# Expert rows with stationary blocks read at a step of two elements, in a fused transformer kernel

## The reference, cut to what matters

```python
expert = (i1 * N_SUB_KEYS + i2)                       # 128 experts for each token, out of 16384
a = jnp.einsum('cd,ced->ce', xb, u_tab[eb])           # up: token . u row
w = gb * jax.nn.gelu(a, approximate=False)            # gate times gelu
out = jnp.einsum('ce,ced->cd', w, v_tab[eb])          # down: sum of v rows
```

## Time and profile before

| | us |
|---|---|
| median of 3 runs | 1674.29 |
| the three runs | 1683.41, 1673.71, 1674.29 |
| the profiled execution's own time | 1680.55 |
| its span, first to last instruction | 1678.8 |
| first and last up-row matmul start | 266.6, 644.9 |
| first down-row matmul to the transposes' start | 646.9, 1017.1 |
| PE busy | 1604.7 (96%) |
| POOL, ACT, DVE busy | 1195.0, 925.4, 882.5 |

### The profile page before, as it was taken

The page is one execution under the profiler, slowest core; times in us unless marked ns, Lnnn a source line. Parts: engine busy times, 40 slices in busy tenths (PEclk is TensorE's granted clock), DMA queues, the critical chain, the costliest instruction groups (busy, mean ns, idle before and its releaser), DMA issues.

```text
span 1678.8 us, 32062 instructions
## 1 busy us (share of the span) xinstructions
PE 1604.7 (96%) x12800; PEld 1466.9 (87%) x12800; DVE 882.5 (53%) x1817; ACT 925.4 (55%) x1553; POOL 1195.0 (71%) x500
## 2 busy tenths in 40 slices
PE   8987999999999999999999999899999998999998
PEld 7876999999999998888888888668999995789997
DVE  6888445993366667777611115678220066762201
ACT  6666655445444445555566656376663445666533
POOL 5552777888877777777888887215988851269885
PEclk9899999999999999999999999899999999999999
DMA  7441555656655555555666665422666644246663
GB/s 255 127 131 45 187 166 177 189 188 188 181 175 175 176 176 175 176 176 169 193 194 193 190 190 160 163 89 93 198 195 193 192 148 151 64 137 204 197 192 112
DMA packets 79891, 280.42 MB, mean 167 GB/s; under 512 B 8704, under 2 KB 9472, under 8 KB 79488
## 3 DMA queue, kind: packets, MB, share of 16 engines
q1 hardware_dynamic: 79744, 278.38, 53.7%
HBM read 277.30 MB, written 1.05 MB: 166 GB/s over the span
## 4 chain that ended last, share of the span: by engine, by line
PE 85%; DVE 7%; issue 3%; ACT 3%; POOL 1%; DMA 1%; DVEq 0%; SPq 0%; ACTq 0%; POOLq 0%
PE ps L2688 14%; PE ps L2048 13%; PE ps L2357 10%; PE ps L2666 7%; PE ps L2695 7%; PE ps L2667 7%; PE ps L2671 7%; PE ps L552 6%; PE ps L2114 1%; POOL wl L213 1%; PE ps L2652 1%; PE ps L2180 1%; PE ps L2654 1%; PE ps L386 1%; PE ps L2150 1%
## 5 line engine op out<-in xcount | busy, mean ns | idle before, releaser
L2466 POOL TENSOR_TENSOR wl<-slots,wh 128x1024 fp32r<-128x1024 f32 x256 | 619.4, 2421 | 129.1 <-ACT wh L2404 126.9
L213 POOL TENSOR_TENSOR wl<-slots,wh 128x1024 fp32r<-128x1024 f32 x178 | 430.5, 2422 | 299.3 <-ACT wh L199 298.7
L2404 ACT ACTIVATE wh<-slots 128x1024 fp32r<-128x1024 f32 x256 | 271.9, 1062 | 355.3 <-issue 231.8
L199 ACT ACTIVATE wh<-slots 128x1024 fp32r<-128x1024 f32 x178 | 188.5, 1060 | 178.4 <-PE ps L2357 63.5
L2666 PE MATMUL ps<-xh,wh 128*128 128x256 f32 x1024 | 244.7, 281 | 0.0
L2667 PE MATMUL ps<-xl,wh 128*128 128x256 f32 x1024 | 241.5, 278 | 0.0
L2666 PEld LDWEIGHTS ps<-xh,wh 128*128 128x128 f32 x1024 | 192.8, 188 | 0.1
L2667 PEld LDWEIGHTS ps<-xl,wh 128*128 128x128 f32 x1024 | 192.9, 188 | 0.0
L213 POOL TENSOR_TENSOR third_lo<-slots,third_hi 128x1024 fp32r<-128x1024 f32 x58 | 141.2, 2434 | 38.8 <-ACT third_hi L199 38.6
L2688 PE MATMUL ps<-wh,xh 128*128 128x512 f32 x508 | 160.5, 397 | 0.0
L2688 PE MATMUL ps<-wh,xl 128*128 128x512 f32 x508 | 157.9, 392 | 0.0
(11 more groups left out here) (428 smaller groups left out, 3421.5 us busy)
## 6 DMA issues: line engine op xcount, KB each, us to landing
slots<-w SPq DMA_DIRECT2D x260, 512.0 KB, 4.1
slots<-wu SPq DMA_DIRECT2D x128, 512.0 KB, 3.6
slots<-wv SPq DMA_DIRECT2D x128, 512.0 KB, 3.6
arena<-bias SPq DMA_DIRECT2D x1, 2048.0 KB, 8.2
h<-xT SPq DMA_DIRECT2D x4, 256.0 KB, 6.3
arena<-keys SPq DMA_DIRECT2D x1, 1024.0 KB, 8.4
yT<-y_out SPq DMA_DIRECT2D x2, 512.0 KB, 2.7
layer<-consts SPq DMA_DIRECT2D x1, 800.0 KB, 5.3
```

The source lines that it names most:

```text
L199: act.activation(self.hi[self.place[n]], self.slots[:, u % SLOTS, :], ACT.Copy).then_inc(self.rounded, 1)
L213: pool.tensor_tensor(self.lo[self.place[n]], self.slots[:, self.order[n] % SLOTS, :], self.hi[self.place[n]].bitcast(F32), ALU.subtract).t ...
L2404: act.activation(whv[:, r % 2, :], slots_v[:, r % SLOTS, :], ACT.Copy).then_inc(w_hi, 1)
L2466: pool.tensor_tensor(wlv[:, r % 2, :], slots_v[:, r % SLOTS, :], whv[:, r % 2, :].bitcast(F32), ALU.subtract).then_inc(w_lo, 1)
```

## The change

The same values are computed and the same number of instructions is issued; only access patterns change.

- Up rows: ACT and POOL write `wh` and `wl` so that two neighbouring chunks of 128 columns lie element by element in turn (column 0 of chunk 0, column 0 of chunk 1, column 1 of chunk 0, ...). ACT reads the slot contiguously and writes with a step of two elements (8 bytes); POOL reads the slot contiguously, reads `wh` and writes `wl` with a step of two. PE's stationary operand is then every second element of a stretch of 256.
- Down rows: the stationary operand takes every second token (`t`, `t + 2`, ...) instead of 128 neighbouring tokens. `wh`, `wl`, `a_hi` and `a_lo` are written as before.
- The 16 transposes behind the down rows write every second column of the PSUM bank, so that the tokens stand in their order again.

```diff
+        def by_pairs(x):
+            return x.rearrange("p (k j n) -> p k j n", k=DC // 2, j=2)
+        def in_turn(x):
+            return x.rearrange("p (k n j) -> p k j n", k=DC // 2, j=2)
...
-                    act.activation(whv[:, r % 2, :], slots_v[:, r % SLOTS, :], ACT.Copy).then_inc(w_hi, 1)
+                    if r < NE2:
+                        ins = act.activation(in_turn(whv[:, r % 2, :]), by_pairs(slots_v[:, r % SLOTS, :]), ACT.Copy)
+                    else:
+                        ins = act.activation(whv[:, r % 2, :], slots_v[:, r % SLOTS, :], ACT.Copy)
+                    ins.then_inc(w_hi, 1)
...
-                    pool.tensor_tensor(wlv[:, r % 2, :], slots_v[:, r % SLOTS, :], whv[:, r % 2, :].bitcast(F32),
-                                       ALU.subtract).then_inc(w_lo, 1)
+                    hi, lo = whv[:, r % 2, :], wlv[:, r % 2, :]
+                    if r < NE2:
+                        ins = pool.tensor_tensor(in_turn(lo), by_pairs(slots_v[:, r % SLOTS, :]),
+                                                 in_turn(hi.bitcast(F32)), ALU.subtract)
+                    else:
+                        ins = pool.tensor_tensor(lo, slots_v[:, r % SLOTS, :], hi.bitcast(F32), ALU.subtract)
+                    ins.then_inc(w_lo, 1)
...
-                    hi, lo = (x[:, r % 2, :].rearrange("p (k n) -> p k n", k=DC) for x in (whv, wlv))
+                    hi, lo = (in_turn(x[:, r % 2, :]) for x in (whv, wlv))
...
-                        pe.matmul(out, hi[:, k, :], xhT[:, k, :], start=(k == 0), stop=False)
-                        ins = pe.matmul(out, hi[:, k, :], xlT[:, k, :], start=False, stop=False)
+                        pe.matmul(out, hi[:, k // 2, k % 2, :], xhT[:, k, :], start=(k == 0), stop=False)
+                        ins = pe.matmul(out, hi[:, k // 2, k % 2, :], xlT[:, k, :], start=False, stop=False)
...
-                        tokens = slice(t * P, (t + 1) * P)
+                        tokens = slice(t, T, TT)
...
-                            ins = pe.matmul(psum[2 * t + half], a_hi[:, t * P:(t + 1) * P],
+                            ins = pe.matmul(psum[2 * t + half], a_hi[:, t:T:TT],
...
-                            ins = pe.transpose(psum[4 + c // 2][:, (c % 2) * T + t * P:(c % 2) * T + (t + 1) * P],
+                            ins = pe.transpose(psum[4 + c // 2][:, (c % 2) * T + t:(c % 2) * T + T:TT],
```

More of the change, by code:

```diff
@@ L2670, in up_row @@
                     for k in range(DC):
-                        ins = pe.matmul(out, lo[:, k, :], xhT[:, k, :], start=False, stop=(k == DC - 1))
+                        ins = pe.matmul(out, lo[:, k // 2, k % 2, :], xhT[:, k, :], start=False, stop=(k == DC - 1))
                     ins.then_inc(lo_done, 1)
```

## The result

The changed kernel takes 1701.8 us (median of 4 runs, 1700.06 to 1705.35). The kernel before takes 1678.85 us (median of 4 runs, 1673.71 to 1684.48: the three runs given above and one more). The ratio is 1.0137 with a 95% interval of 1.0113 to 1.0162: the change makes the kernel 23 us, or 1.4%, slower. Forecast were 34.5 us less, and a range from 1628 to 1692 us.

The account below looks back on a forecast made before the run. PE was taken as the bound, busy 96% of the span. Savings of 20.0 us (down rows), 7.5 and 7.0 us (up rows), together 34.5, gave 1646 us against the profiled execution, 1640 against the median; range 1628 to 1692 us.

Parts of the forecast that it names:

- Removed: the stalls above: Up and down rows: read collisions vanish, down matmuls 229 to 216 ns, up matmuls to 110; 34.5 us saved.
- POOL at 2.42 us: Rows' POOL instructions with a step of 8 bytes stay at 2.42 us, with 0.2 us to spare in an up row.
- ACT unchanged: Up rows' 128 roundings written with a step of two: 1.06 us now, covered even at double that; cost nothing.
- Transposes at nothing: Behind the down rows, 16 transposes writing every second PSUM column: between no cost and 1.8 us; taken as 0.
- Grids, DMA: Row pairs 5% shorter, DVE's grid work stays covered; weight loads at 202 GB/s against 193 cost nothing.
- The sign for more collisions: Down rows taking above 2.9 us each would mean that a step of two collides more.
- one mechanism: The reading explains up and down rows alike; it fails if the two kinds move in opposite directions.
- More stalls: Rival, chance 0.10: blocks over twice the memory double the rows' excess above 110 and 216 ns; 1709 us, half 1691.
- No change: Rival, chance 0.13: excess belongs to the moving stream or PSUM write, so stationary layout does not matter; 1674 us.
- Half of it: Rival, chance 0.12: only down rows gain, or up rows with some down stalls; 14 to 20 us less, 1654 to 1660.
- POOL becomes the bound: Rival, chance 0.13: up rows' strided POOL instructions become the limit; at 3.4 us each the kernel takes 1709 us.
- 40 rows at 117.8: Some 40 up rows, about 298 to 411 us, lose 7.8 ns a matmul that the change removes: 7.5 us.

Follow-up runs that it names:

- e8: Against the kernel before, down rows 1 to 126 use 64 of 128 tokens as stationary block; down pace 228.3 ns, down stage 366.1 us.
- e4: Against the kernel before, PE reads the up rows' stationary blocks with a step of two from contiguously written data; 1702.8 us.
- e6: Against the kernel before, 22 of 24 matmuls of an up row move 128 of 256 columns; loads every 112 ns.
- e7: Against the changed kernel, 22 of 24 matmuls of an up row move 128 of 256 columns; loads every 120 ns.
- e16: Against the kernel before, up rows' stationary blocks read at a step of three from contiguous data; 1865.46 us.
- e5: Against the kernel before, up rows' stationary blocks read at a step of four from contiguous data; 2048.81 us.

## Why the prediction was wrong

**The step that failed** is the first term, "Removed: the stalls above". It rested on the inference that two reads of different speed run into each other and that two of equal speed do not, and it took the whole excess above plain float32's 2.7 ns for removable. The runs show three errors in it. First, most of the excess does not depend on how much is loaded: 113.3 ns with 64 stationary columns as with 128, and 228.3 against 228.9 in the down rows. Second, the loads do slow the matmul beside them, but through how a block is strided and where the weights lie, and equal speeds do not help: step two costs 4.4 ns a late down matmul, 1536 x 4.4 ns = 6.8 us, measured 6.2. Third, the floor of an up matmul by its load was taken as 110 ns from contiguous blocks. That figure was nearly right for them (112), but a strided block needs 120, and then the load is the bound: 88 rows x 24 x (120.0 - 113.3) plus 40 rows x 24 x (120.0 - 117.8) = 14.2 + 2.1 = 16.3 us, measured 15.2. The sum is +23.1 us in place of -34.5; the two traces differ by 21.4. The price of a strided load was the unknown of this change; I gave POOL and ACT a range for the step and PE's load none.

**Point by point.** That PE is the bound and that nothing else would wait held. POOL at 2.42 us: 2.49 (the median of its up rows is 2.46), within the room of 0.2 us. ACT unchanged: 1.16 instead of 1.06, hidden as said. Transposes at nothing: held. Grids, DMA: held. One reading of the windows was wrong without a consequence: between 310 and 400 us DVE, busy 80.11 of 90 us, came next after PE, not POOL with 78.08. The sign for more collisions was set too high: down rows every 2.80 us, not above 2.9. And both kinds of rows moved the same way, which the prediction would have read as one mechanism; in the up rows the load's own length came on top of what the down rows show. The plain float32 rows, which I read as "equal speeds do not collide", are explained just as well by the moving side being half as fast. In no kernel here was that told apart; it stays open, and so does what the excess of the kernel before consists of.

**The rivals.** *More stalls* named the right direction and roughly the right property, a block spread over twice the memory, and its 1709 us (1691 at half) brackets 1701.8. That is partly luck. Its mechanism fits the down rows, at a third of the size (4.4 ns, not 13), and what is left in the up rows when the load is halved (4 ns); but the up rows run at 120 because the load itself is longer, which it does not have. *No change* had one half of the truth, that the excess belongs to the moving stream (or to its write into PSUM, which no run tells apart); it missed the loads. By the Trainium skill (TensorE: Matmul & The Clock Gate, Step-by-step: what each phase is for) loading weights takes no read bandwidth from the running matmul; the down rows at 228.3, 231.1 and 233.3 ns with the same moving operand do not agree, and the measurement decides. *Half of it* and *POOL becomes the bound* did not happen.

The loads themselves: by the Trainium skill (TensorE: Matmul & The Clock Gate, LDWEIGHTS (loading the stationary operand)) a load's price goes by its columns alone, 107 ns for 128, an estimate from it; the traces have 112, 120, 175 and 235 ns at steps of one to four. The Trainium skill (SBUF — State Buffer, the note on 16-byte cachelines under Door 1: The DMA port swizzle) asks for two hits in each 16-byte line. The steps of three and four bear that out, and at a step of two, where each line has its two hits, the load still takes 7% more than a contiguous one (120 against 112 ns). In the up rows the load had only 1% to spare (112 against 113.3 ns), so the 7% showed.

**The 117.8 stretches.** I counted 40 rows at 117.8 as removable. They do not belong to particular rows or to the work beside them: the stretch is shorter and lies elsewhere in the down-only and writes-only kernels, whose up reads are unchanged (up stages of 378.0 and 377.0 us against 380.2), it is absent in e8, whose up rows are those of the kernel before (376.0), and in e4 a stretch of the second block, which the edit does not touch, ran at 140 us / 1192 = 117.4 ns instead of 140 / 1238 = 113.1:

```profile
1200.00:1340.00 140.00, 140.00 (x1192) 140.00 (x1191) 19.25 (x30) 69.54 (x82) 120.83 (x51) 1.00 0.62 191
```

```profile
1200.00:1340.00 140.00, 140.00 (x1238) 140.00 (x1237) 14.86 (x23) 66.95 (x75) 124.05 (x53) 1.00 0.65 194
```

The first line is e4's, the second the kernel's before. What selects the pace is not settled. In the traces it changes where the stream of matmuls is broken: in the kernel before it goes to 117.8 at 302.4 us, where two matmuls start 217 and 225 ns apart behind a long POOL instruction, and back to 113.3 at 414 us, behind six transposes.

## What to carry to other kernels

Where matmuls of 256 moving columns of rounded float32 follow each other, the load of the next block takes about as long as the matmul (112 against 113.3 ns here): price the load's access pattern before anything else, and keep such stationary blocks contiguous. An unexplained excess over the columns' time is not yet a cost that a layout can remove; first cut the suspected partner in half and see whether it moves. And when a change shifts tensors in SBUF, compare it with a kernel in which only the shift is done: here 16 bytes cost as much as the change.

## What the runs showed of the hardware

- A stationary block of 128 columns of rounded float32 comes every 112, 120, 175 or 235 ns at steps of 1, 2, 3 and 4 elements (e6, e7, e16, e5).
- A strided load slows the matmul beside it even where it is far shorter than that matmul: 64 columns at a step of two take a 512-column matmul from 228.3 to 231.1 ns, 64 at a step of four to 233.3.
- Rounded float32 with 256 moving columns runs at 113.3 ns, also when only 64 stationary columns are loaded; at half of the 0.84 ns a column that the plain float32 rows show, its columns would need 107 (an estimate).
- Moving the weights by 16 to 48 bytes against the rest costs 4.4 ns on a 229 ns matmul and 28 to 38 us on the kernel. Why one of four places is good is not explained.
- The same instructions run at 113.3 or at 117.8 ns for hundreds of matmuls on end, in different stretches of different runs. The second block of e4, with a stretch of some 170 us at the slower pace, took 9 us more than that of the kernel before (672.0 us after the rows against 662.9); the runs of the kernel before differ among themselves by 11.
- ACT pays 9% for writing 1024 elements with a step of two (1.16 against 1.06 us), POOL 2.5% for reading and writing with it (2.46 against 2.40 us, medians).
